# Expert weights with four lines per partition, bf16 parts in natural column order, and a re-ordered router and last pass

## The reference

```python
h2 = rmsnorm(x, norm2_g) * (1 + sc2) + sh2
pg = softmax(h2 @ rg_w + rg_b)                 # 4 groups, best one
le = (h2 @ re_w + re_b)[group of the token]    # 8 experts of it, best two
y  = sum_e weight_e * ((silu(h2 @ w1[e]) * (h2 @ w3[e])) @ w2[e])
x  = x + gt2 * y ;  out = rmsnorm(x, final_g)
```

## Time and profile before

| | |
|---|---|
| runs | 1869.19, 1870.86 (median), 1872.15 us |
| profiled execution | 1872.05 us, span 1870.3 us |
| busy in the span: TensorE matmul, weight load | 1768.9 us (95%), 1006.2 us (54%) |
| busy: VectorE, ScalarE, GpSimd | 899.9 us (48%), 397.0 us (21%), 0.8 us |
| DMA | 642.00 MB, mean 343 GB/s |
| mean granted TensorE clock | 0.977 |

### The profile page before, as it was taken

How to read it: one execution, slowest core, us unless ns; L and a number is a source line. 1 busy time by engine, 2 the same in 40 slices (tenths; PEclk the granted TensorE clock), 3 DMA queues, 4 the chain that set the end, 5 groups by cost and what they waited for, 6 DMA issues and landing times.

```text
span 1870.3 us, 26150 instructions
## 1 busy us (share of the span) xinstructions
PE 1768.9 (95%) x10310; PEld 1006.2 (54%) x10310; DVE 899.9 (48%) x1088; ACT 397.0 (21%) x482; POOL 0.8 (0%) x5
## 2 busy tenths in 40 slices
PE   1979999999999999999999999999999999999995
PEld 1868747786777777686434434434343433333341
DVE  5877766866758644356433333323333332333333
ACT  3010023432323233334211101111011111101112
POOL 0000000000000000000000000000000000000000
PEclk8889999999999999999999999999999999999998
DMA  9996597879878834455499999999999999999994
GB/s 373 387 387 249 203 383 268 313 283 348 311 268 300 336 135 180 157 213 227 198 422 422 422 422 422 422 422 422 422 422 422 422 422 422 422 422 422 423 421 198
DMA packets 136716, 642.00 MB, mean 343 GB/s; under 512 B 8546, under 2 KB 8674, under 8 KB 76130
## 3 DMA queue, kind: packets, MB, share of 16 engines
q1 hardware_dynamic: 135968, 637.08, 85.5%
q10 hardware_dynamic: 562, 2.63, 0.4%
q0 software_dynamic: 144, 1.70, 0.2%
HBM read 639.28 MB, written 2.10 MB: 343 GB/s over the span
## 4 chain that ended last, share of the span: by engine, by line
PE 60%; DMA 29%; DVE 7%; issue 1%; ACT 1%; DVEq 1%; SPq 0%; ACTq 0%
DMA ring<-in_exp_w 24%; PE ps L930 14%; PE ps L894 5%; PE ps L656 5%; PE ps L658 5%; PE ps L657 5%; PE ps L626 5%; DVE r_m L1262 4%; PE ps L569 3%; PE ps L582 3%; PE ps L917 2%; DMA ring<-in_branch_w 2%; DMA ring<-in_ada_w 2%; PE ps L756 2%; PE ps L757 2%; PE ps L758 2%
## 5 line engine op out<-in xcount | busy, mean ns | idle before, releaser
L930 PE MATMUL ps<-ring 128*64 128x512 f32 x2048 | 466.5, 597 | 11.6 <-DMA ring<-in_exp_w 11.6
L930 PEld LDWEIGHTS ps<-ring 128*64 128x64 f32 x2048 | 144.0, 137 | 299.1 <-issue 299.0
L1639 DVE TENSOR_TENSOR r_h<-r_h,ps 128x1024 f32<-128x1024 f32 x128 | 150.6, 1218 | 213.5 <-PE ps L917 213.4
L657 PE MATMUL ps<-g_lo,h_hi 128*128 128x512 f32 x512 | 201.9, 394 | 0.0
L1612 DVE TENSOR_TENSOR r_c<-ps,scale 128x512 f32<-128x512 f32 x65 | 44.7, 688 | 292.9 <-PE ps L872 292.5
L1188 ACT ACTIVATE r_m<-ps 128x512 f32<-128x512 f32 x32 | 19.1, 597 | 705.3 <-PE ps L930 705.3
L656 PE MATMUL ps<-mix_hi,h_hi 128*128 128x512 f32 x384 | 158.4, 412 | 0.0
L1073 ACT ACTIVATE mix_hi<-ring 128x1024 fp32r<-128x1024 f32 x96 | 101.7, 1062 | 262.1 <-PE ps L658 262.1
L1369 DVE TENSOR_TENSOR g_lo<-ring,mix_hi 128x1024 fp32r<-128x1024 f32 x96 | 117.5, 1225 | 78.3 <-ACT mix_hi L1073 77.5
L658 PE MATMUL ps<-mix_hi,h_lo 128*128 128x512 f32 x384 | 152.3, 397 | 0.0
L917 PE MATMUL ps<-ring,r_m 64*128 64x512 f32 x512 | 127.5, 615 | 1.4 <-DVE ring L1632 1.0
(11 more groups left out here) (260 smaller groups left out, 1742.2 us busy)
## 6 DMA issues: line engine op xcount, KB each, us to landing
ring<-in_exp_w SPq DMA_DIRECT2D x320, 1024.0 KB, 21.8
ring<-in_w_in SPq DMA_DIRECT2D x40, 2048.0 KB, 10.0
r_b<-in_exp_w SPq DMA_DIRECT2D x64, 1024.0 KB, 24.4
ring<-in_ada_w SPq DMA_DIRECT2D x24, 2048.0 KB, 19.0
ring<-in_ada_w SPq DMA_DIRECT2D x48, 1024.0 KB, 5.1
ring<-in_w_o SPq DMA_DIRECT2D x8, 2048.0 KB, 7.7
ring<-in_w_in SPq DMA_DIRECT2D x12, 1024.0 KB, 14.9
ring<-in_branch_w SPq DMA_DIRECT2D x6, 2048.0 KB, 9.6
```

The costliest lines, as they stand in the source:

```text
L657: mm(ps[:, b + t, :], h, lo[:, cols], start=False, stop=False)
L930: last = mm(ps[m * NWIN:(m + 1) * NWIN, 2, :], xe[:, k, :], chunk(2 * c + m)[:, kk * F:(kk + 1) * F], start=(k == 0), stop=(k == KT - 1))
L1639: V.tensor_tensor(x1n, x1n, ps[:, (6, 4)[b]:(6, 4)[b] + 2, :].rearrange("p b n -> p (b n)"), ALU.add).then_inc(added, 1)
```

## The change

The order of channels changes: block (c, j) holds the channels 512c + 4q + j. So partition q needs 4 adjacent lines of each quarter of w1 and w3, and the transposes of the router can use the same order as the experts. `fan`, `tall` and line 692 go. The bf16 parts keep the natural column order of x1, and the gather's stationary tiles are read 4 bf16 apart. TensorE's order in the router, ScalarE's with it, and all behind the loop are re-written: the last pass has functions of its own, and the final norm and store work in halves. Table loads are called forth early by small activations. The host's constants and the orders of `wide` and `router_w` follow.

```diff
@@ -106,7 +104,7 @@
-x1_k = x1.rearrange("p t (q k) -> p t k q", k=KT)
+x1_k = x1.rearrange("p t (c q j) -> p t c j q", c=4, j=4)
@@ -155,13 +153,13 @@
+xparts_k = xparts[:, :, :, :].rearrange("p i t (c q j) -> p i t c j q", c=4, j=4)
...
-fan = r_c[:, 3072:3328].rearrange("p (v a b) -> p v a b", v=2, a=8)
@@ -316,8 +315,8 @@
-e1_v = exp_w1.rearrange("e (p k) n -> e p k n", p=P)
-e3_v = exp_w3.rearrange("e (p k) n -> e p k n", p=P)
+e1_v = exp_w1.rearrange("e (c p j) n -> e p c j n", c=4, p=P)
+e3_v = exp_w3.rearrange("e (c p j) n -> e p c j n", c=4, p=P)
@@ -464,7 +463,7 @@
-                         w[bass.ds(e, 1), :, 4 * c:4 * c + 4, :].rearrange("e p k n -> (e p) k n")
+                         w[bass.ds(e, 1), :, c, :, :].rearrange("e p j n -> (e p) j n")
@@ -503,9 +502,12 @@
-        sp.wait_ge(fin_ready, t + 1)
-        sp.dma_start(out_v[:, t, :], slot(2)[:, t * D:(t + 1) * D]).then_inc(out_done, 16)
-    sp.wait_ge(out_done, 32)
+        for b in range(2):
+            sp.wait_ge(fin_ready, 2 * t + b + 1)
+            cols = slice(2 * b * MIX, (2 * b + 2) * MIX)
+            sp.dma_start(out_v[:, t, cols], slot(2)[:, t * D + 2 * b * MIX:t * D + (2 * b + 2) * MIX]
+                         ).then_inc(out_done, 16)
+    sp.wait_ge(out_done, 64)
@@ -528,7 +530,7 @@
-    acc_k = acc.rearrange("p (q k) -> p k q", k=KT)
+    acc_k = acc.rearrange("p (c q j) -> p c j q", c=4, j=4)
@@ -684,13 +686,8 @@
-            part = acc[:, k * P:(k + 1) * P] if SH2 + g == GT2 else acc_k[:, k, :]
+            part = acc[:, k * P:(k + 1) * P] if SH2 + g == GT2 else acc_k[:, k // 4, k % 4, :]
             last = mm(ps[:, 6, k:k + 1], part, ones[:, 0:1], start=True, stop=True)
-        if SH2 + g == GT2:
-            pe.wait_ge(fan_ready, 1)
-            for i in range(2):
-                last = mm(ps[:, 6, 32 + i * KT:32 + (i + 1) * KT], fan[:, i, :, :], keep[:, K_OCT:K_OCT + KT],
-                          start=True, stop=True)
@@ -789,7 +786,7 @@
-                                       x1[:, t, n * MIX + k * P:n * MIX + (k + 1) * P], ident)
+                                       x1_k[:, t, n, k, :], ident)
@@ -817,7 +814,7 @@
-        mm(ps[:, bank, :], root_diag[t], x1_k[:, t, 4 * b:4 * b + 4, :], start=True, stop=False,
+        mm(ps[:, bank, :], root_diag[t], x1[:, t, b * MIX:(b + 1) * MIX], start=True, stop=False,
@@ -832,9 +829,6 @@
-    pe.wait_ge(logit_read, 1)
-    for b in range(2):
-        first_rest(1, b, 2 + b)
@@ -845,14 +839,13 @@
+    first_rest(1, 0, 2)
     pe.wait_ge(cnt_ready, 1)
     mm(ps[:, 0, 128:160], ct[:, 0, :], tri[0:32, 0:32], start=True, stop=True).then_inc(start_done, 1)
+    first_rest(1, 1, 3)
...
-    for b in range(4):
-        second_rest(1, b, (2, 3, 4, 5)[b])
@@ -861,6 +854,8 @@
+    for b in range(4):
+        second_rest(1, b, 2 + b)
@@ -869,7 +864,7 @@
-                    last = mm(gat[:, kk, :], xparts[:, i, t, k * P:(k + 1) * P], chosen[:, t, 0:NWIN],
+                    last = mm(gat[:, kk, :], xparts_k[:, i, t, k // 4, k % 4, :], chosen[:, t, 0:NWIN],
@@ -977,11 +972,38 @@
+    def last_second(b):
+        for f in range(FT):
+            if b == 0:
+                pe.wait_ge(w2_in[f], 16 * n_pass)
+            for side in range(2):
+                q = 2 * b + side
+                last = mm(ps[side * NWIN:(side + 1) * NWIN, 4 + b, :], hid[:, f, :],
+                          chunk(CHUNKS + f)[:, q * MIX:(q + 1) * MIX], start=(f == 0), stop=(f == FT - 1))
+        last.then_inc(half_done, 1)
+    def last_combine(t, b, bank):
+        pe.wait_ge(ye_saved, 2 * n_pass + b + 1)
+        for side in range(2):
+            half = slice(side * NWIN, (side + 1) * NWIN)
+            last = mm(ps[:, bank + side, :], pair_wT[half, t * P:(t + 1) * P], y_sb[half, b, :],
+                      start=True, stop=True)
+        last.then_inc(tail_comb, 1)
     turn(n_pass)
+    pe.wait_ge(hid_ready, n_pass)
+    pe.wait_ge(added, 4 * n_pass + 1)
+    last_second(0)
     turn_weights(n_pass)
-    second(n_pass, 0, FT)
-    for i in range(4):
-        combine(n_pass, i)
+    last_second(1)
+    pe.wait_ge(wT_ready, n_pass + 1)
+    last_combine(0, 0, 6)
+    last_combine(1, 0, 2)
+    last_combine(0, 1, 0)
+    pe.wait_ge(tail_added, 1)
+    last_combine(1, 1, 6)
@@ -1126,7 +1148,7 @@
-        A(xparts[:, 0, t, :].rearrange("p (k q) -> p k q", k=KT), x1_k[:, t, :, :], ACT.Copy,
+        A(xparts[:, 0, t, :], x1[:, t, :], ACT.Copy,
@@ -1141,6 +1163,7 @@
+    A(stat[:, 20:21], keep[:, K_EPS:K_EPS + 1], ACT.Sqrt).then_inc(warm_up, 1)
@@ -1151,11 +1174,9 @@
-    for b in range(2):
-        part_mid(1, b, 2 + b)
     for b in range(4):
         part_low(0, b, 4 + b)
-    for b in range(2, 4):
+    for b in range(4):
@@ -1202,18 +1223,31 @@
+    A(stat[:, 20:21], keep[:, K_EPS:K_EPS + 1], ACT.Silu).then_inc(warm_up, 1)
     silu(n_pass)
     copy_weights(n_pass)
-    for t in range(TT):
-        for n in range(4):
-            act.wait_ge(added, 4 * n_pass + 2 + 2 * t + n // 2)
-            if t:
-                act.wait_ge(sq_done, 6 + n + 1)
-            A(squares[:, n * MIX:(n + 1) * MIX], x1[:, t, n * MIX:(n + 1) * MIX], ACT.Square,
-              accum_out=stat[:, 8 + 4 * t + n:9 + 4 * t + n]).then_inc(sq_done, 1)
+    A(stat[:, 21:22], keep[:, K_EPS:K_EPS + 1], ACT.Sqrt).then_inc(warm_up, 1)
+    def square(i):
+        b, t = i // 2, i % 2
+        act.wait_ge(tail_added, (1, 2, 3, 4)[i])
+        if i >= 2:
+            act.wait_ge(sq_done, 6 + i - 1)
+        cols = slice(2 * b * MIX, (2 * b + 2) * MIX)
+        A(squares[:, t * 1024:(t + 1) * 1024], x1[:, t, cols], ACT.Square,
+          accum_out=stat[:, 8 + 2 * t + b:9 + 2 * t + b]).then_inc(sq_done, 1)
+    def last_root(t):
         act.wait_ge(inv_ready, 5 + t)
         A(stat[:, 16 + t:17 + t], stat[:, 16 + t:17 + t], ACT.Sqrt).then_inc(root_done, 1)
+    for i in range(3):
+        square(i)
+    last_root(0)
+    square(3)
+    last_root(1)
@@ -1436,19 +1470,9 @@
-    branch_gate(1, False)
-    save_mod(SC2, 6)
-    v.wait_ge(mod_ready, 7)
-    step(V.scalar_tensor_tensor(out=scale2[:, :], in0=mod[:, SC2, :], scalar=1.0, in1=col[:, C_N2:C_N2 + KT],
-                                op0=ALU.add, op1=ALU.mult))
-    spread = keep[:, K_FAN:K_FAN + P].rearrange("p (a b) -> p a b", a=8)
-    step(V.tensor_tensor(fan[:, 0, :, :], spread, mod[:, SH2, :].unsqueeze(1).broadcast_to([P, 8, KT]), ALU.mult))
-    V.tensor_tensor(fan[:, 1, :, :], spread, scale2[:, :].unsqueeze(1).broadcast_to([P, 8, KT]), ALU.mult
-                    ).then_inc(fan_ready, 1)
-    branch_gate(2, False)
-    v.wait_ge(summed, GT2 + 7)
-    step(V.tensor_copy(tall[:, :, :], ps[:, 6, 32:64].rearrange("p (v k) -> p v k", v=2)))
-    save_mod(GT2, 6)
+    for g in range(1, N_BRANCH - 1):
+        branch_gate(g, False)
+        save_mod(SH2 + g, 6)
@@ -1463,10 +1487,12 @@
+    step(V.scalar_tensor_tensor(out=scale2[:, :], in0=mod[:, SC2, :], scalar=1.0, in1=col[:, C_N2:C_N2 + KT],
+                                op0=ALU.add, op1=ALU.mult))
     step(V.memset(rws[:, :, 36:NWIN], 0.0))
-    step(V.tensor_tensor(rws[:, :, 0:36], rw, by_k(tall[:, 0, :]), ALU.mult))
+    step(V.tensor_tensor(rws[:, :, 0:36], rw, by_k(mod[:, SH2, :]), ALU.mult))
     step(V.tensor_reduce(cst_k[:, :], rws[:, :, 0:36].rearrange("p c n -> p n c"), AX_X, ALU.add))
-    V.tensor_tensor(rws[:, :, 0:36], rw, by_k(tall[:, 1, :]), ALU.mult).then_inc(rw_scaled, 1)
+    V.tensor_tensor(rws[:, :, 0:36], rw, by_k(scale2[:, :]), ALU.mult).then_inc(rw_scaled, 1)
@@ -1527,7 +1553,6 @@
-    v.sem_inc(logit_read, 1)
@@ -1685,28 +1710,52 @@
+    hidden(n_pass)
     last_off = v.value_load(otab[0:1, bass.ds(n_pass, 1)], min_val=0, max_val=PAIRS)
     window(n_pass, last_off)
-    hidden(n_pass)
-    for b in range(2):
-        save_output(n_pass, b)
-    for i in range(4):
-        add_moe(n_pass, i)
+    def last_output(b):
+        v.wait_ge(half_done, b + 1)
+        V.tensor_tensor(y_sb[:, b, :], ps[:, 4 + b, :], gt2row[:, b, :], ALU.mult).then_inc(ye_saved, 1)
+    def last_add(t, b, bank, count):
+        v.wait_ge(tail_comb, count)
+        x1n = x1[:, t, 2 * b * MIX:(2 * b + 2) * MIX]
+        V.tensor_tensor(x1n, x1n, ps[:, bank:bank + 2, :].rearrange("p b n -> p (b n)"), ALU.add
+                        ).then_inc(tail_added, 1)
+    last_output(0)
+    last_output(1)
+    last_add(0, 0, 6, 1)
+    last_add(1, 0, 2, 2)
+    last_add(0, 1, 0, 3)
+    last_add(1, 1, 6, 4)
     v.wait_ge(fg_in, 16)
-    def last_norm(t):
-        v.wait_ge(sq_done, 6 + 4 * (t + 1))
+    def last_mean(t):
+        v.wait_ge(sq_done, 6 + 3 + t)
         r = stat[:, 16 + t:17 + t]
-        step(V.tensor_reduce(r, stat[:, 8 + 4 * t:12 + 4 * t], AX_X, ALU.add))
+        step(V.tensor_reduce(r, stat[:, 8 + 2 * t:10 + 2 * t], AX_X, ALU.add))
         step(V.tensor_scalar(r, r, 1.0 / D, EPS, ALU.mult, ALU.add))
         V.reciprocal(r, r).then_inc(inv_ready, 1)
+    def scaled(t, b):
         v.wait_ge(root_done, 5 + t)
```

(31 more changed lines are left out.)

## The result

The changed kernel takes 1860.49 us (1858.33 to 1861.73), the kernel before on the same chip 1870.53 (1869.19 to 1872.15): a ratio of 0.9945, 95% interval 0.9931 to 0.9958, a gain of 10 us where 17.5 were forecast. The profiled execution of after is its fastest (1858.33, span 1856.5), that of before lay above its median; so 13.7 us lie between the two profiles, 3.7 more than between the medians.

The account below looks back on a forecast made before the run. Expert-weight loads at 422 GB/s were taken to bound the late passes, with TensorE in reserve. Gate stage -7.1, router -6.3 and tail -4.1 gave -17.5 us: forecast 1853, own range 1847 to 1859, 8-in-10 range 1846 to 1930.

Parts of the forecast that it names:

- the first rival: Gather, line 872: the tile load's pace doubles, 30 ns more on 2976 tiles, total 1926 us; chance 0.18.
- The gate stage: Column sums ahead of the router: steps of 4 instead of 16 and line 692 gone, -7.1 us, bounds -4 to -9.
- At 0.117 us each they take 3.75 us: Gate stage, column sums of SH2 and SC2 at four apart, priced from line 881's loads; saves 6.3 us.
- The ladder "16 bytes cost 7%, 64 bytes a doubling": fp32 stationary loads: line 881 and router transposes gave 7% at 16 bytes, line 688's sums the doubling at 64.
- The router: Adjacent columns shorten first-rest steps from 1.94 to 1.08 us and counts start earlier: -6.3 us, bounds -3 to -8.
- The tail: Behind the loop: earlier second product, overlapped norm by halves, smaller last store: -4.1 us, bounds -2.5 to -5.5.
- The gather: Expert passes, bf16 tiles read 8 bytes apart: 2 ns a tile, 6 us in all, hidden in the reserve, visible cost 0.
- the reserve of 15.8: TensorE's slack in 18 load-held expert passes, 0.88 us each, 15.8 us in all, which the gather may spend.
- The 7%: fp32 cost of a 16-byte step, taken as the likely upper end for the gather's 8 bytes: 2 ns a tile.
- The expert stream: Loads of w1 and w3 as unbroken megabytes: rate stays 422 GB/s, cost 0, bound 0 to -15.8 us.
- Rival (3): Expert stream gets faster from unbroken megabytes and TensorE never waits: another -15.8 us, 1837; chance 0.04.
- Rival (4): Gate stage held by its loads, router by ScalarE; half of 13.4 us goes: 1860; chance 0.06.

Follow-up runs that it names:

- The wide products: Changed kernel, all three column sums as ordinary fp32 products with the 128-column identity, reduced on VectorE, instead of one-column products: 1857.54 us, ratio 0.9928.
- the turned sums: Column sums as 16 transposes plus VectorE reduction: all three on the changed kernel, 1840.65 us; first two on the kernel before, 1855.17 us.
- the timed pairs: Old code behind the loop put back: on the changed kernel 1862.37 us against 1860.49; on the turned sums 1845.08 against 1840.65.

## Why the prediction was right, and where it was not

The direction and the bound held, and the first rival did not come. The sum missed by 7.5 us, and most of that is one term. The measured 1860.49 lies outside the forecast's own 1847 to 1859; it is inside 1846 to 1930 only because that range was stretched upward to hold the gather's doubling, which did not come. That is luck, not foresight.

**The gate stage, -7.1 forecast, 0 to 2.5 us gained** (what the timed 10 us leave beside the router and the tail; by the single executions about 0). **This is the step that failed.** "At 0.117 us each they take 3.75 us" took a price from the transposes at line 881 and gave it to the products of the sums. Measured: 0.233 us a record four apart, 0.216 sixteen apart, 0.111 adjacent at the upper clock. The ladder "16 bytes cost 7%, 64 bytes a doubling" was read across two kinds of operation; neither kind by itself shows it. Transposes pay 10% at 16 bytes and 4% at 64, products with their two records a tile double at both. The wide products show that the kind decides and not the column count, the turned sums at both steps that transposes escape. The rows of before held a hint: the stepped sums were known to double, and only a row of another kind said that a smaller step would heal them. What was gained on the third sum (0.85 by line 692, which went as forecast, and 0.13) went to the first two (0.5 each). The rest of the range that the prediction left open, 2 us either way by the clock, is what single executions scatter by.

**The router, -6.3 forecast, -5.6 measured.** A step of 1.08 us was forecast, 1.07 measured; VectorE's wait goes to 0.93; then ScalarE is late by 1.30 us ahead of the gather's first half, which the prediction had excluded. The matmul that stood at line 951 comes 6.3 us earlier, as forecast, and 0.7 are lost behind it. Taking that wait away gave 0.6 of them back in the router and nothing in the whole.

**The tail, -4.1 forecast,** 3.2 to 4.5 in the profiles, 1.9 and 4.4 in the timed pairs. The product started 1.8 us earlier (1.9 forecast).

**The gather, 2 ns a tile forecast, 4.3 measured** (48 loads took 1.68 us, where 1.46 to 1.6 were to be seen). 2976 x 4.3 = 12.8 us of loads, not 6. Of these the passes show 31 x 0.22 = 6.8, and 6.0 went into the wait at line 899 (8.2 us adjacent, 2.2 in after), which the prediction did not know of. So 6.8 us of the reserve of 15.8 were spent. That is close to the forecast 6 by luck: the price was twice as high, and half of it was hidden. 14 held passes of 29.82 - 29.17 leave 9.1. The 7% was one of transposes again. For bf16, what the Trainium skill says of two hits a line (SBUF — State Buffer, Specifications), which the sum did without, would have been the better ground. The first rival's doubling did not come at 8 bytes but is real at 16, with its time: 1934, where the rival said 1926. The Trainium skill (TensorE: Matmul & The Clock Gate, Weight-path perf modes) says that such loads read 32 bits at a time. What the prediction made of it, twice the time at 8 bytes, is not borne out: 33.7 ns.

**The expert stream, 0:** 422 GB/s and 29.82 us in both, and the old views of w1 and w3 give the same time. Rival (3) is out. Rival (4), 1860 with early gains eaten, gives the measured number but not its cause: the gate stage was not held by its loads, since the turned sums moved its end by 19 us, and it had no gain to eat. ScalarE held the router by 0.7 us.

Not settled: why a product's tile with two records doubles by a step while a transpose's does not, and why the stepped one does not care for the clock; no run here looks into a load. And what sets the start of the clock's low stretches from one execution to the next.

## What to carry to other kernels

Price a step in a stationary tile only from rows with the same kind of operation and the same type; a transpose says nothing on a product. For bf16 tiles a step of 8 bytes cost 4 ns and one of 16 bytes 31, and no run lies between: keep to 8. Before calling a price hidden, look for every wait that it can fall into. And look at short products on the path for what they do behind themselves: here a column sum with one moving column cost its own 7.5 us, then some 2 at the lower clock, then a late load behind the first, and turning it into transposes with a reduction on an idle engine brought twice what the whole change did.

## What the hardware did that was not expected

- fp32 products load a tile in 0.111 us a record adjacent, 0.233 with a step of 16 bytes and 0.216 with 64: the smaller step is the dearer one. fp32 transposes: 0.109, 0.121 and 0.113, in the same order.
- The stepped products take 0.233 and 0.216 us a record at either level of the clock; adjacent ones take 0.111 at the upper and 0.213 at the lower.
- bf16 tiles: 29.4, 33.7, 60.7 and 63.2 ns from one gather matmul to the next, at 2, 8, 16 and 32 bytes.
- With 32 records of one moving column (7.5 us) the granted clock fell to 0.50, its lower level, while they ran, and stayed there for up to 6 us behind them; with 32 equally long records of 128 moving columns it stayed at 1.00. With the 3.5 us of the third, adjacent sum it fell in the execution of before and not in that of after.
- VectorE's fp32 operation on 512 columns: 1131 ns with one input four apart and the other and the output adjacent, 752 with all adjacent.
